# Expert hidden activations turned on VectorE instead of TensorE, and the final-row work moved around them

## The chip, the cores and the metric

The kernel runs on one core of one Trainium2 chip. The core has five engines with a queue each: TensorE (PE; its weight loads are listed as PEld), VectorE (DVE), ScalarE (ACT), GpSimd (POOL) and SyncE (SP). Engines run their own instructions in order and meet at semaphores. The metric is device time in microseconds (us) of one launch. The kernel before took 2361.81 us, the median of three runs (2359.26, 2361.81, 2366.89).

## The reference, cut to what matters

One encoder layer is applied to two groups of 1024 rows of width 1024. Its last part is an expert-choice mixture: each of 16 experts picks 128 rows of each group.

```python
gate, idx = lax.top_k(aff.T, cap)                 # cap = 128 rows of a group, for each expert
xe = xf[idx]
hid = silu(xe @ w_gate[e]) * (xe @ w_up[e])       # per expert, 1024 wide
ye = (hid @ w_down[e]) * gate
y = zeros.at[idx].add(ye)                         # rows of all experts added up
x = x + gate2 * rmsnorm(y)                        # the final rows
```

All matrices are f32. The kernel splits each operand into a high and a low part and forms each product from three matmuls (high by high, low by high, high by low).

## The kernel before, in words

The function `experts` covers the second half of the time, from about 1283 us on. It runs experts 0 to 15 in turn; the first eight stand in a loop, the last eight are written out. Both groups are worked on together: 128 rows of each.

**Weights.** An expert has three matrices, called GATE, UP and DOWN, and each comes in four pieces of 1 MB. Four buffers hold pieces. SP loads a piece (`moe_wf`), ACT copies its high part (`moe_w_hi`, line 2404), DVE subtracts to get the low part (`moe_w_lo`, line 2553), and PE multiplies with both (line 2734). A "split" is the ACT copy and the DVE subtraction of one piece. A buffer is free for the next split when PE has finished the piece four places earlier.

**Order on PE** in the body of expert e: UP(e), GATE(e+1), DOWN(e), twelve pieces of 24 matmuls. GATE(e+1) waits for the turned and split inputs of expert e+1 (`x_ready`, `moe_x_lo`, line 2573).

**Hidden activations.** ACT writes silu of the GATE sums to `hid`, DVE multiplies them by the UP sums (line 2598). DOWN needs `hid` turned, rows against columns. For experts 0 to 7 DVE turns it with 16 transposes (line 2581), ACT and DVE then split it from SBUF (lines 2423 and 2587), and PE does the high parts of DOWN's first piece ahead of the low parts (`down_first`, line 2766). For experts 8 to 15 (`is_late`) PE turns it with 16 transposes in the midst of GATE(e+1) (line 2754), and ACT and DVE split it out of PSUM (lines 2411 and 2559).

**Inputs of an expert.** POOL gathers the rows of expert e+2 with eight indirect DMAs (line 2308), DVE turns them (line 2568). POOL also adds an expert's output rows to `scratch_y` in HBM with two indirect DMAs (line 2325, the "scatter").

**Final rows.** 26 units of 128 rows are finished while experts 9 to 15 still run, four to an expert (two in expert 15), in pairs. For a unit POOL loads rows of y and of x1 (lines 2337 and 2338; 2341 and 2342 where the rows are picked by an index), ACT sums the squares (line 2458, it waits for the y load), DVE makes the mean (2602), POOL the root (2352), DVE the result (2610 and 2616, the latter waits for the x1 load), and POOL stores it (2359, by index 2365). Units 0 to 15 are plain rows, units 16 to 25 go by index. Units use buffers 0 and 1 in turn; a load waits until the store two units earlier has landed. A POOL body starts when the scatter of the expert before has landed: loads of the first pair, gather of one group, roots, stores, then the same for the second pair, then the scatter. Units 26 and 27, the rows of expert 15, end the kernel.

Of the kernel before, what the change touches and what calls it, by code (L numbers as in the profile page):

```python
# [8 lines left out]
ALU = mybir.AluOpType  # L9
# [24 lines left out]
ONE = 1  # L34
# [2054 lines left out]
def experts(nc, io):  # L2089
# [5 lines left out]
    NP = KC // PIECE  # L2095
# [8 lines left out]
    LATE = 8  # L2104
# [15 lines left out]
    with ExitStack() as ctx:  # L2120
# [64 lines left out]
        late_h_turned, late_h_hi_ready, late_h_ready = (s.sem(f"late_h_{n}") for n in ("turned", "hi_ready", "ready"))  # L2185
# [46 lines left out]

        def is_late(e):
            return isinstance(e, int) and e >= LATE

# [29 lines left out]
        def _(pool):  # L2265
# [65 lines left out]
            def load_unit(n):  # L2331
# [4 lines left out]
                if t is not None:  # L2336
                    pool.dma_start(fy[:, j, :], y_view[t]).then_inc(fy_loaded[j], 16)
                    pool.dma_start(fx[:, j, :], x1_view[t]).then_inc(fx_loaded[j], 16)
                else:
                    at = bass.IndirectOffsetOnAxis(ap=index_c[:, col(e, g)], axis=0)  # L2340
                    pool.indirect_dma_start(fy[:, j, :], None, io["y"], at).then_inc(fy_loaded[j], 16)  # L2341
# [8 lines left out]
            def root(n):  # L2350
                pool.wait_ge(y_mean, n + 1)
                nc.gpsimd.tensor_tensor(y_r[:, n % 2:n % 2 + 1], y_ss[:, n % 2:n % 2 + 1], mhalf[:, :], ALU.pow).then_inc(y_root, 1)
# [44 lines left out]
        def _(act):  # L2397
# [27 lines left out]
            def silu(e, j, bs=range(BK)):  # L2425
# [4 lines left out]
                if len(bs) == BK and is_late(e - 1):  # L2430
                    act.wait_ge(late_h_turned, ONE + (e - LATE) * BK)
                elif len(bs) == BK:
                    act.wait_ge(h_turned, ONE + e)
# [38 lines left out]
            def body(e, j):  # L2472

                ns = window(e)
                if is_last(e):
                    split(e, DOWN, range(0, 2))
                    turned_out(e - LATE, (h_hi, j), late_h_turned, late_h_hi_ready, range(0, 2))
# [3 lines left out]
                    turned_out(e - LATE, (h_hi, j), late_h_turned, late_h_hi_ready, range(2, BK))  # L2481
                else:
# [30 lines left out]
        def _(dve):  # L2513
# [119 lines left out]
            def body(e, j):  # L2633
                ns = window(e)
                if is_last(e):
                    multiply(e, j, range(0, 2))
                    split(e, DOWN, range(0, 2))
                    turned_out(e - LATE, h_hi, h_lo, j, late_h_hi_ready, late_h_ready, range(0, 2))
                    multiply(e, j, range(2, BK))
                    split(e, DOWN, range(2, NP))  # L2640
                    for n in ns:
                        mean(n)
                    turned_out(e - LATE, h_hi, h_lo, j, late_h_hi_ready, late_h_ready, range(2, BK))
                    for n in ns:
                        result(n)
                else:
# [3 lines left out]
                    if is_late(e):  # L2650
                        split(e + 1, GATE, range(2, NP))
                        multiply(e, j)
                    else:
                        split(e + 1, GATE, range(2, 3))
                        multiply(e, j)
                        split(e + 1, GATE, range(3, NP))
                        turn_h(e)
                    split(e, DOWN, range(0, 1))
                    if not is_late(e):
                        h_out(e)  # L2660
                    for n in ns[0:2]:
                        mean(n)
                    split(e, DOWN, range(1, 2))
                    if is_late(e):
                        turned_out(e - LATE, h_hi, h_lo, j, late_h_hi_ready, late_h_ready)
# [232 lines left out]
```

## Time and profile before

| | us |
|---|---|
| median of three runs | 2361.81 |
| the profiled execution | 2362.63 |
| its span, first to last instruction | 2360.9 |
| PE busy | 2255.7 (96%) |
| DVE busy | 1349.1 (57%) |
| ACT busy | 1100.5 (47%) |
| POOL busy | 730.6 (31%) |

Times in rows count from the start of the span. The profiled execution's own time is 1.7 us more than its span. A row of the timeline gives the start, the duration, engine, line, what is written from what, and in brackets the idle time of that engine before it with what ended it. A DMA's row on POOL tells how long POOL took to issue it, not when the data landed; landing times stand in the views of one line.

### The profile page before, as it was taken

Reading aid. Unit: us, or ns where it says so; the run is one execution under the profiler, and the core shown is the slowest. Engines: PE = TensorE matmul, PEld = TensorE weight load, DVE = VectorE, ACT = ScalarE, POOL = GpSimd, SP = SyncE. Lnnn points to the kernel's source line nnn. Section 1 sums busy time; section 2 is a strip of 40 time slices with the busy share of each in tenths; the row PEclk is TensorE's granted clock in tenths of the full one; section 3 lists DMA queues with packets and bytes.
Section 4 is the critical chain, followed back from the end, with each engine's and each line's share of the span. In section 5 each row is a group of like instructions: output and inputs, shape, how many; then the busy total and the mean of one; then the engine's idle time right before and its main releaser. Section 6 shows DMA issues by size and latency. Waiting matters only on the chain. (4 is left out here: it accounts for less than half of the span.)

```text
span 2360.9 us, 34620 instructions
## 1 busy us (share of the span) xinstructions
PE 2255.7 (96%) x13219; PEld 1876.9 (79%) x13219; DVE 1349.1 (57%) x1995; ACT 1100.5 (47%) x1782; POOL 730.6 (31%) x770
## 2 busy tenths in 40 slices
PE   6999999999999999999984999999999999999997
PEld 4679989867899898677763888888888888888885
DVE  3212344555422436665557877777777667677665
ACT  4212434555534436665542544544444455545552
POOL 3004241434233515340003222221222333443634
PEclk9999999999999999999996999999999999999998
DMA  8745445657554459764538666766667678988785
GB/s 314 265 114 184 153 148 192 188 137 185 139 188 152 148 172 247 225 183 162 169 128 313 215 218 231 248 223 224 209 224 244 229 267 316 334 311 302 286 304 178
DMA packets 224095, 511.49 MB, mean 217 GB/s; under 512 B 38420, under 2 KB 129444, under 8 KB 204496
## 3 DMA queue, kind: packets, MB, share of 16 engines
q1 hardware_dynamic: 174576, 394.78, 49.3%
q0 software_dynamic: 49376, 114.78, 16.5%
q8 instruction: 92, 1.51, 0.3%
q14 instruction: 51, 0.42, 0.1%
HBM read 415.32 MB, written 93.69 MB: 216 GB/s over the span
## 5 line engine op out<-in xcount | busy, mean ns | idle before, releaser
L2553 DVE TENSOR_TENSOR moe_w_lo<-moe_wf,moe_w_hi 128x2048 fp32r<-128x2048 f32 x192 | 437.2, 2288 | 252.4 <-ACT moe_w_hi L2404 251.5
L2404 ACT ACTIVATE moe_w_hi<-moe_wf 128x2048 fp32r<-128x2048 f32 x192 | 366.0, 1915 | 436.7 <-PE moe_acc L2734 424.1
L2734 PE MATMUL moe_acc<-moe_w_hi,moe_x_hi 128*128 128x512 f32 x1024 | 400.1, 391 | 2.9 <-DVE moe_w_lo L2553 2.0
L2734 PE MATMUL moe_acc<-moe_w_lo,moe_x_hi 128*128 128x512 f32 x1024 | 399.2, 390 | 0.0
L2734 PE MATMUL moe_acc<-moe_w_hi,moe_x_lo 128*128 128x512 f32 x1024 | 399.1, 390 | 0.0
L2734 PEld LDWEIGHTS moe_acc<-moe_w_hi,moe_x_hi 128*128 128x128 f32 x1024 | 192.6, 188 | 43.7 <-DVE moe_w_lo L2553 2.4
L2734 PEld LDWEIGHTS moe_acc<-moe_w_hi,moe_x_lo 128*128 128x128 f32 x1024 | 192.6, 188 | 40.1
L2734 PEld LDWEIGHTS moe_acc<-moe_w_lo,moe_x_hi 128*128 128x128 f32 x1024 | 192.5, 188 | 39.7
L1793 PE MATMUL banks<-fr_w_hi,fr_h_hi 128*128 128x256 f32 x768 | 223.2, 291 | 0.0
L1793 PE MATMUL banks<-fr_w_lo,fr_h_hi 128*128 128x256 f32 x768 | 217.0, 283 | 0.0
L1793 PE MATMUL banks<-fr_w_hi,fr_h_lo 128*128 128x256 f32 x768 | 216.9, 282 | 0.0
L2308 POOL DMA_INDIRECT moe_xe<-scratch_h,moe_parts x120 | 181.5, 1513 | 86.8 <-issue 77.3
L1784 PE MATMUL banks<-fr_h_hi,fr_w_hi 128*128 128x512 f32 x496 | 204.3, 412 | 1.9 <-DVE fr_h_lo L1381 1.1
L1784 PE MATMUL banks<-fr_h_hi,fr_w_lo 128*128 128x512 f32 x496 | 194.2, 392 | 0.0
L1784 PE MATMUL banks<-fr_h_lo,fr_w_hi 128*128 128x512 f32 x496 | 193.7, 391 | 0.0
L1030 ACT ACTIVATE fr_stage<-banks 128x512 f32<-128x512 f32 (+1 forms) x114 | 67.4, 591 | 270.9 <-PE banks L1784 145.8
L1362 DVE TENSOR_TENSOR fr_w_lo<-fr_w_raw,fr_w_hi 128x1024 fp32r<-128x1024 f32 x56 | 71.2, 1274 | 209.3 <-ACT fr_w_hi L1018 209.3
L906 POOL DMA_DIRECT2D fr_v<-scratch_vov x224 | 156.2, 746 | 81.9 <-PE banks L1963 80.5
L2734 PE MATMUL moe_acc<-moe_w_hi,moe_h_hi 128*128 128x512 f32 x448 | 174.4, 389 | 0.0
L2734 PE MATMUL moe_acc<-moe_w_hi,moe_h_lo 128*128 128x512 f32 x448 | 174.3, 389 | 0.0
L2734 PE MATMUL moe_acc<-moe_w_lo,moe_h_hi 128*128 128x512 f32 x448 | 174.3, 389 | 0.0
L1793 PEld LDWEIGHTS banks<-fr_w_hi,fr_h_hi 128*128 128x128 f32 x768 | 146.8, 191 | 4.9 <-issue 4.8
(312 smaller groups left out, 4306.7 us busy)
## 6 DMA issues: line engine op xcount, KB each, us to landing
moe_wf<-in_w_expert_gate SPq DMA_DIRECT2D x64, 1024.0 KB, 5.3
moe_wf<-in_w_expert_up SPq DMA_DIRECT2D x64, 1024.0 KB, 6.0
moe_wf<-in_w_expert_down SPq DMA_DIRECT2D x64, 1024.0 KB, 6.8
fr_w_raw<-in_w_units SPq DMA_DIRECT2D x28, 1024.0 KB, 6.7
fr_bias<-in_na_bias SPq DMA_DIRECT2D x16, 1520.0 KB, 11.7
fr_a_w<-in_w_ada POOLq DMA_DIRECT2D x16, 1024.0 KB, 8.4
scratch_qk_t<-fr_stage SPq DMA_DIRECT2D x64, 256.0 KB, 2.5
scratch_vov<-fr_stage SPq DMA_DIRECT2D x96, 128.0 KB, 2.4
```

Source lines behind the costliest of these rows:

```text
L906: pool.dma_start(v[j][p0:CHUNK, CH_AT[rb] + n, :], v_view[2, m, r0:r0 + k, cols_, :]).then_inc(nv_loaded[j], 16)
L1030: nc.scalar.activation(out, product, ACT.Copy).then_inc(evac_done, 1)
L1362: nc.vector.tensor_tensor(w_lo[:, h % 2, k, :], w_raw[:, h % 2, k, :], w_hi[:, h % 2, k, :].bitcast(F32), ALU.subtract).then_inc(w_lo_read ...
L1784: mm = nc.tensor.matmul(ps[:, b % 2, :], w[x1][:, slot, k, a * P:(a + 1) * P], h[x2][:, k, t * HALF:(t + 1) * HALF], start=start, stop=stop)
L1793: mm = nc.tensor.matmul(ps[:, b % 2, part * QW:(part + 1) * QW], h[x1][:, k, tile:tile + P], w[x2][:, slot, k, :], start=(k == 0 and i == ...
L2308: pool.indirect_dma_start(quarter_rows(g)[:, t, :], None, h2_quarters, bass.IndirectOffsetOnAxis(ap=at, axis=0)).then_inc(gathered[g], 16)
L2404: nc.scalar.activation(w_hi[:, q, :, :], wf[:, q, :, :], ACT.Copy).then_inc(w_hi_ready, 1)
L2553: nc.vector.tensor_tensor(w_lo[:, q, :, :], wf[:, q, :, :], w_hi[:, q, :, :].bitcast(F32), ALU.subtract).then_inc(w_lo_ready, 1)
L2734: mm = nc.tensor.matmul(acc[:, j, b, :], x[:, g, k, :], w[:, q, a, h * HALF:(h + 1) * HALF], start=(k == 0 and i == 0), stop=(k == KC - 1 ...
```

## The change

`LATE` and `is_late` go: experts 8 to 14 turn `hid` as experts 0 to 7 do, by DVE, and PE transposes it for expert 15 alone. The rest moves the work on final rows. POOL's gather of both groups comes first in the body, before the wait for the scatter. A pair's two y loads are issued together, and without waiting for the stores of the pair before; the x1 loads follow, with that wait. On ACT and DVE the squares, means and results of a pair stand one split later.

```diff
-                if not ns and not is_last(e, 2):
+                if not is_last(e, 2):
                     gather(e + 2, j)
                 if ns:
                     pool.wait_ge(added, (ZEROS + e * GROUPS) * 16)
-                    for h, half in enumerate((ns[0:2], ns[2:4])):
+                    for half in (ns[0:2], ns[2:4]):
                         for n in half:
-                            load_unit(n)
-                        if not is_last(e, 2):
-                            gather(e + 2, j, range(h, h + 1))
+                            load_y(n)
+                        for n in half:
+                            load_x1(n)
```

`load_y` has no wait; `load_x1` begins with the old one:

```diff
+            def load_x1(n):
+                j = n % 2
+                g, t, e = units[n]
+                if n >= 2:
+                    pool.wait_ge(out_stored[j], 16 * (n // 2))
```

ACT, body of an expert that is not the last:

```diff
                     split(e, DOWN, range(0, 1))
-                    if not is_late(e):
-                        h_out(e)
+                    h_out(e)
+                    split(e, DOWN, range(1, 2))
                     for n in ns[0:2]:
                         square(n)
-                    split(e, DOWN, range(1, 2))
-                    if is_late(e):
-                        turned_out(e - LATE, (h_hi, j), late_h_turned, late_h_hi_ready)
                     split(e, DOWN, range(2, NP))
 
                     silu(e + 1, 1 - j)
-                    split(e + 1, UP, range(0, 2))
+                    split(e + 1, UP, range(0, 3))
                     for n in ns[2:4]:
                         square(n)
-                    split(e + 1, UP, range(2, NP))
+                    split(e + 1, UP, range(3, NP))
```

DVE, the end of the same body:

```diff
                     for n in ns[0:2]:
                         result(n)
-                    split(e, DOWN, range(2, NP))
-                    split(e + 1, UP, range(0, 2))
+                    split(e, DOWN, range(3, NP))
+                    split(e + 1, UP, range(0, 3))
                     for n in ns[2:4]:
                         mean(n)
+                    split(e + 1, UP, range(3, NP))
                     for n in ns[2:4]:
                         result(n)
-                    split(e + 1, UP, range(2, NP))
```

PE, the same body:

```diff
-                    products(e + 1, GATE, 1 - j, x_hi[:, 1 - j], x_lo[:, 1 - j], first)
-                    if is_late(e):
-                        turn_h(e, j)
-                    products(e + 1, GATE, 1 - j, x_hi[:, 1 - j], x_lo[:, 1 - j], second)
-                    if is_late(e):
-                        pe.wait_ge(late_h_ready, ONE + (e - LATE) * BK + BK)
-                        products(e, DOWN, j, h_hi, h_lo)
-                    else:
-                        down_first(e, j)
-                        products(e, DOWN, j, h_hi, h_lo, range(1, NP))
+                    products(e + 1, GATE, 1 - j, x_hi[:, 1 - j], x_lo[:, 1 - j])
+                    down_first(e, j)
+                    products(e, DOWN, j, h_hi, h_lo, range(1, NP))
```

In the last expert DVE's means of its two units come behind the split of the second half of `hid` instead of ahead of it; ACT's squares stay ahead of that half's copy out of PSUM.

Where it moves instructions, first on DVE around `hid` of a late expert. Before, from the multiplication (`moe_hid`) on; `moe_w_lo` is a weight split, `moe_parts` the means, `moe_h_lo` the split of the turned `hid`:

```order
L2598 TENSOR_TENSOR moe_hid<-moe_hid,moe_acc 128x512 x4
L2553 TENSOR_TENSOR moe_w_lo<-moe_wf,moe_w_hi 128x2048
L2602 TENSOR_SCALAR moe_parts<-moe_parts 128x1 x2
L2553 TENSOR_TENSOR moe_w_lo<-moe_wf,moe_w_hi 128x2048
L2559 TENSOR_TENSOR moe_h_lo<-moe_acc,moe_h_hi 128x512 x4
```

Now, at the same place (lines lie one lower):

```order
L2597 TENSOR_TENSOR moe_hid<-moe_hid,moe_acc 128x512 x4
L2552 TENSOR_TENSOR moe_w_lo<-moe_wf,moe_w_hi 128x2048
L2580 STREAM_TRANSPOSE moe_h_raw<-moe_hid 32x16x32 x16
L2552 TENSOR_TENSOR moe_w_lo<-moe_wf,moe_w_hi 128x2048
L2586 TENSOR_TENSOR moe_h_lo<-moe_h_raw,moe_h_hi 128x1024 x2
L2552 TENSOR_TENSOR moe_w_lo<-moe_wf,moe_w_hi 128x2048
L2601 TENSOR_SCALAR moe_parts<-moe_parts 128x1 x2
```

Sixteen transposes have come in, the split of `hid` is two instructions on SBUF instead of four on PSUM, and the means stand behind a weight split more.

Second, DVE at the end of the body, from DOWN's last splits to the turn of the next expert's inputs (`moe_x_raw`). Before:

```order
L2553 TENSOR_TENSOR moe_w_lo<-moe_wf,moe_w_hi 128x2048 x4
L2602 TENSOR_SCALAR moe_parts<-moe_parts 128x1 x2
L2610 SCALAR_TENSOR_TENSOR moe_fy<-moe_fy,moe_parts,moe_rows 128x1024
L2616 TENSOR_TENSOR moe_fx<-moe_fx,moe_fy 128x1024
L2610 SCALAR_TENSOR_TENSOR moe_fy<-moe_fy,moe_parts,moe_rows 128x1024
L2616 TENSOR_TENSOR moe_fx<-moe_fx,moe_fy 128x1024
L2553 TENSOR_TENSOR moe_w_lo<-moe_wf,moe_w_hi 128x2048 x2
L2568 STREAM_TRANSPOSE moe_x_raw<-moe_xe 128x4x8x32 x2
```

Now:

```order
L2552 TENSOR_TENSOR moe_w_lo<-moe_wf,moe_w_hi 128x2048 x4
L2601 TENSOR_SCALAR moe_parts<-moe_parts 128x1 x2
L2552 TENSOR_TENSOR moe_w_lo<-moe_wf,moe_w_hi 128x2048
L2609 SCALAR_TENSOR_TENSOR moe_fy<-moe_fy,moe_parts,moe_rows 128x1024
L2615 TENSOR_TENSOR moe_fx<-moe_fx,moe_fy 128x1024
L2609 SCALAR_TENSOR_TENSOR moe_fy<-moe_fy,moe_parts,moe_rows 128x1024
L2615 TENSOR_TENSOR moe_fx<-moe_fx,moe_fy 128x1024
L2567 STREAM_TRANSPOSE moe_x_raw<-moe_xe 128x4x8x32 x2
```

The second pair's two results stand between the body's last weight split and the turn of the next inputs; two weight splits stood there.

Third, POOL in expert 13, whose units go by index: loads (`moe_fy` is y, `moe_fx` is x1), gather (`moe_xe`), roots (`moe_parts`), stores (`out`). Before:

```order
L2341 DMA moe_fy<-scratch_y,moe_parts 128x1024
L2342 DMA moe_fx<-scratch_x,moe_parts 128x1024
L2341 DMA moe_fy<-scratch_y,moe_parts 128x1024
L2342 DMA moe_fx<-scratch_x,moe_parts 128x1024
L2308 DMA moe_xe<-scratch_h,moe_parts 128x256 x4
L2352 TENSOR_TENSOR moe_parts<-moe_parts 128x1 x2
L2365 DMA out<-moe_fx,moe_parts 2048x1024 x2
```

Now:

```order
L2304 DMA moe_xe<-scratch_h,moe_parts 128x256 x8
L2334 DMA moe_fy<-scratch_y,moe_parts 128x1024 x2
L2345 DMA moe_fx<-scratch_x,moe_parts 128x1024 x2
L2356 TENSOR_TENSOR moe_parts<-moe_parts 128x1 x2
L2369 DMA out<-moe_fx,moe_parts 2048x1024 x2
```

The whole gather is ahead of the loads, and the y loads are next to each other.

## Rows read from the trace of the kernel before

**Rows 1.** The page, busy time of each engine, share and instructions.

```profile
PE 2255.7 (96%) x13219; PEld 1876.9 (79%) x13219; DVE 1349.1 (57%) x1995; ACT 1100.5 (47%) x1782; POOL 730.6 (31%) x770
```

**Rows 2.** Chain that ended last, from 1840 us: start, us, what.

```profile
1861.34 1.75 PE moe_acc L2754 x16
1863.09 65.31 PE moe_acc L2734 x288
```

**Rows 3.** Waits of PE from 1861 us on: total us, times, longest.

```profile
PE moe_acc L2734 <- DVE moe_w_lo L2553: 2.0, 1, 2.0
```

**Rows 4.** Timeline of PE at the start of UP(15) and at its stall.

```profile
2297.98 0.39 PE L2734 MATMUL moe_acc<-moe_w_hi,moe_x_hi 128*128 128x512 f32 x1
...
2305.56 0.61 PE L2734 MATMUL moe_acc<-moe_w_hi,moe_x_hi 128*128 128x512 f32 x1 [1.98 <-DVE moe_w_lo L2553]
...
2309.55 0.40 PE L2734 MATMUL moe_acc<-moe_w_lo,moe_x_hi 128*128 128x512 f32 x1
```

**Rows 5.** Busy us by stretch (PE, PEld, DVE, ACT, POOL), clock, DMA share, GB/s.

```profile
1632.60:1697.90 65.30, 65.30 (x290) 54.07 (x289) 49.40 (x38) 30.84 (x24) 16.06 (x13) 1.00 0.67 225
...
2263.70:2330.80 67.10, 65.12 (x298) 53.83 (x295) 40.95 (x33) 33.10 (x34) 31.23 (x18) 0.97 0.71 242
```

**Rows 6.** Timeline of DVE in expert 5, whose UP starts at 1632.6.

```profile
1637.06 4.19 DVE L2568 STREAM_TRANSPOSE moe_x_raw<-moe_xe 128x1024 f32<-128x1024 f32 x2
...
1645.73 2.29 DVE L2553 TENSOR_TENSOR moe_w_lo<-moe_wf,moe_w_hi 128x2048 fp32r<-128x2048 f32 x1 [2.31 <-ACT moe_w_hi L2404]
1647.93 2.35 DVE L2573 TENSOR_TENSOR moe_x_lo<-moe_x_raw,moe_x_hi 128x1024 fp32r<-128x1024 f32 x2
...
1654.66 2.48 DVE L2598 TENSOR_TENSOR moe_hid<-moe_hid,moe_acc 128x512 f32<-128x512 f32 x4 [1.14 <-PE moe_acc L2734]
...
1659.43 11.45 DVE L2581 STREAM_TRANSPOSE moe_h_raw<-moe_hid 32x512 f32<-32x512 f32 x16
...
1673.12 2.35 DVE L2587 TENSOR_TENSOR moe_h_lo<-moe_h_raw,moe_h_hi 128x1024 fp32r<-128x1024 f32 x2
```

**Rows 7.** Timeline of DVE, a result's first half, then last halves of three pairs.

```profile
2002.10 1.28 DVE L2610 SCALAR_TENSOR_TENSOR moe_fy<-moe_fy,moe_parts,moe_rows 128x1024 f32<-128x1024 f32 x1
...
2207.15 1.23 DVE L2616 TENSOR_TENSOR moe_fx<-moe_fx,moe_fy 128x1024 f32<-128x1024 f32 x1
...
2277.34 1.23 DVE L2616 TENSOR_TENSOR moe_fx<-moe_fx,moe_fy 128x1024 f32<-128x1024 f32 x1
...
2302.08 1.23 DVE L2616 TENSOR_TENSOR moe_fx<-moe_fx,moe_fy 128x1024 f32<-128x1024 f32 x1
```

**Rows 8.** Timeline of ACT: a weight split and a square.

```profile
2019.10 1.92 ACT L2404 ACTIVATE moe_w_hi<-moe_wf 128x2048 fp32r<-128x2048 f32 x1 [3.52 <-PE moe_acc L2734]
2021.10 1.06 ACT L2458 ACTIVATE moe_zero<-moe_fy 128x1024 f32<-128x1024 f32 x1
```

**Rows 9.** Line 2337, the 14 plain y loads from 1937 to 2146 us.

```profile
DMA to landing us min/median/max: 5.8/7.7/10.4
```

**Rows 10.** Timeline of POOL behind the first pair of experts 13 and 14.

```profile
2208.66 2.77 POOL L2365 DMA_INDIRECT out<-moe_fx,moe_parts  x1 [0.68 <-DVE moe_fx L2616]
2211.73 2.76 POOL L2341 DMA_INDIRECT moe_fy<-scratch_y,moe_parts  x1 [0.30 <-issue]
...
2281.92 1.90 POOL L2341 DMA_INDIRECT moe_fy<-scratch_y,moe_parts  x1 [0.30 <-issue]
```

**Rows 11.** Line 2341, landing of the loads issued at 2211.73 and 2281.92.

```profile
DMA to landing us min/median/max: 11.5/11.5/11.5
...
DMA to landing us min/median/max: 9.7/9.7/9.7
```

**Rows 12.** Timelines of POOL and DVE at the end.

```profile
2321.17 2.40 POOL L2341 DMA_INDIRECT moe_fy<-scratch_y,moe_parts  x1 [8.83 <-DMA scratch_y<-moe_ye,moe_parts]
...
2334.97 1.11 POOL L2352 TENSOR_TENSOR moe_parts<-moe_parts 128x1 f32<-128x1 f32 x2
...
2349.93 1.28 DVE L2703 SCALAR_TENSOR_TENSOR moe_ye<-moe_fy,moe_parts,moe_ye 128x1024 f32<-128x1024 f32 x1 [0.76 <-POOL moe_parts L2352]
```

More of the change, by code:

```diff
@@ L2103, in experts @@
     FIRST, UNITS = 8, 4
-    LATE = 8
     units = [(t // TT, t, None) for t in range(GROUPS * TT)]
@@ L2184, in experts @@
         hid_ready = s.sem("hid_ready")
-        late_h_turned, late_h_hi_ready, late_h_ready = (s.sem(f"late_h_{n}") for n in ("turned", "hi_ready", "ready"))
+        last_h_turned, last_h_hi_ready, last_h_ready = (s.sem(f"last_h_{n}") for n in ("turned", "hi_ready", "ready"))
         h_turned = s.sem("h_turned")
@@ L2231, in quarter_rows @@
             return xe[:, g, :].rearrange("p (t n) -> p t n", t=4)
-        def is_late(e):
-            return isinstance(e, int) and e >= LATE
         def is_last(e, n=1):
@@ L2329, in _, with load_y @@
             gather(1, 1)
-            def load_unit(n):
+            def load_y(n):
+                j = n % 2
+                g, t, e = units[n]
+                if t is not None:
+                    pool.dma_start(fy[:, j, :], y_view[t]).then_inc(fy_loaded[j], 16)
+                else:
+                    at = bass.IndirectOffsetOnAxis(ap=index_c[:, col(e, g)], axis=0)
+                    pool.indirect_dma_start(fy[:, j, :], None, io["y"], at).then_inc(fy_loaded[j], 16)
+            def load_x1(n):
                 j = n % 2
@@ L2350, in root @@
             def root(n):
+                mean = y_ss[:, n % 2:n % 2 + 1]
                 pool.wait_ge(y_mean, n + 1)
-                nc.gpsimd.tensor_tensor(y_r[:, n % 2:n % 2 + 1], y_ss[:, n % 2:n % 2 + 1], mhalf[:, :], ALU.pow).then_inc(y_root, 1)
+                nc.gpsimd.tensor_tensor(y_r[:, n % 2:n % 2 + 1], mean, mhalf[:, :], ALU.pow).then_inc(y_root, 1)
             def store_unit(n):
@@ L2429, in silu @@
                     act.wait_ge(piece_done, ONE + piece(e, GATE, NP))
-                if len(bs) == BK and is_late(e - 1):
-                    act.wait_ge(late_h_turned, ONE + (e - LATE) * BK)
-                elif len(bs) == BK:
+                if len(bs) == BK:
                     act.wait_ge(h_turned, ONE + e)
@@ L2476, in body @@
                     split(e, DOWN, range(0, 2))
-                    turned_out(e - LATE, (h_hi, j), late_h_turned, late_h_hi_ready, range(0, 2))
+                    turned_out(0, (h_hi, j), last_h_turned, last_h_hi_ready, range(0, 2))
                     split(e, DOWN, range(2, NP))
@@ L2480, in body @@
                         square(n)
-                    turned_out(e - LATE, (h_hi, j), late_h_turned, late_h_hi_ready, range(2, BK))
+                    turned_out(0, (h_hi, j), last_h_turned, last_h_hi_ready, range(2, BK))
                 else:
@@ L2637, in body @@
                     split(e, DOWN, range(0, 2))
-                    turned_out(e - LATE, h_hi, h_lo, j, late_h_hi_ready, late_h_ready, range(0, 2))
+                    turned_out(0, h_hi, h_lo, j, last_h_hi_ready, last_h_ready, range(0, 2))
                     multiply(e, j, range(2, BK))
                     split(e, DOWN, range(2, NP))
+                    turned_out(0, h_hi, h_lo, j, last_h_hi_ready, last_h_ready, range(2, BK))
                     for n in ns:
                         mean(n)
-                    turned_out(e - LATE, h_hi, h_lo, j, late_h_hi_ready, late_h_ready, range(2, BK))
                     for n in ns:
@@ L2649, in body @@
                     x_out(e + 1, 1 - j)
-                    if is_late(e):
-                        split(e + 1, GATE, range(2, NP))
-                        multiply(e, j)
-                    else:
[L2654 to L2657, printed above, removed]
+                    split(e + 1, GATE, range(2, 3))
+                    multiply(e, j)
+                    split(e + 1, GATE, range(3, NP))
+                    turn_h(e)
                     split(e, DOWN, range(0, 1))
-                    if not is_late(e):
-                        h_out(e)
+                    h_out(e)
+                    split(e, DOWN, range(1, 2))
                     for n in ns[0:2]:
                         mean(n)
-                    split(e, DOWN, range(1, 2))
-                    if is_late(e):
-                        turned_out(e - LATE, h_hi, h_lo, j, late_h_hi_ready, late_h_ready)
+                    split(e, DOWN, range(2, 3))
                     for n in ns[0:2]:
                         result(n)
-                    split(e, DOWN, range(2, NP))
-                    split(e + 1, UP, range(0, 2))
+                    split(e, DOWN, range(3, NP))
+                    split(e + 1, UP, range(0, 3))
                     for n in ns[2:4]:
                         mean(n)
+                    split(e + 1, UP, range(3, NP))
                     for n in ns[2:4]:
                         result(n)
-                    split(e + 1, UP, range(2, NP))
             over_experts(dve, body)
```

11 lines of the change are left out of this document (3 added, 8 removed).

## The prediction

> **What bounds the kernel now.** The busy times of the page came first: PE works 96% of the span [rows 1]. The chain of waits came next. From 1840 us it runs through PE alone, a stretch of 288 matmuls in 65.31 us and then 1.75 us for 16 transposes, five times over [rows 2]; so a matmul takes 65.31 / 288 = 0.2268 us, one of the twelve pieces of an expert 5.44 us, and a late expert 67.06 us. The reader should see that nothing stands between: the view of waits has one wait of PE behind 1861 us, 2.0 us [rows 3]. It is in UP(15): UP(15) begins at 2297.98, the gap is at 2305.56, and the ten matmuls up to 2309.55 then take 3.99 us instead of 2.27 [rows 4]. That is 1.7 us more, with a granted clock of 0.97 in that stretch against 1.00 elsewhere [rows 5], which is some matmuls at the lower of the two levels, 1.2 instead of 2.4 GHz, after PE had idled. So up to expert 14 PE sets the pace, and every instruction taken off it counts in full, provided that DVE, ACT and POOL keep up. From the end of PE's work a tail of DVE and POOL steps follows [rows 12].
>
> **PE: what goes.** Experts 8 to 14 lose 16 transposes each: 7 x 1.75 = 12.2 us, all on the path. That the other form costs PE nothing by itself shows in expert 5, which turns by DVE: PE is busy 65.30 of 65.30 us there [rows 5].
>
> **DVE in an expert with final rows.** I lay it out in time t from the start of UP(e) on PE: GATE(e+1) begins at 21.8, DOWN(e) at 43.5, the next UP at 65.3. Expert 5 started at 1632.6 (expert 8's transposes at 1861.34, less six pieces and three experts). There the inputs' turn starts at t = 4.5, their low parts end at 17.7, the 16 transposes (11.45 us) end at 38.3, the low parts of `hid` at 42.9 [rows 6]. Now two results, 2 x (1.28 + 1.23) = 5.0 us [rows 7], stand ahead of that turn. The turn then ends at 13.7, two weight splits at 18.1, and the low parts of the inputs at 20.4; the 2.31 us that DVE idled there in expert 5 [rows 6] takes up part. PE wants them at 21.8: 1.3 us of cover. Behind it, a split (22.6) and the multiplication (25.0, half a microsecond behind expert 5's) put the low parts of `hid` at 43.4, and `down_first` wants them only after two thirds of a piece, at 47.2. This part costs nothing, and is bounded by the 1.3 us: any delay of the second results beyond it is a wait of PE.
>
> **Where the second results stand.** The split of DOWN's second piece ends at 45.7. ACT's copies of the high parts (from t = 38.3), that copy, two squares and the third piece's copy (1.92 and about 1.25 us each [rows 8]) let DVE end its third split at 49.7, and the first pair's results at 54.7. POOL stores, then loads y for the second pair without a wait. ACT can start the squares when its copy for UP's third piece is done, at 61.9 (eleven pieces of PE and 1.92), and must end them by 65.4, when DOWN is done and the last copy can start.
>
> For plain rows (units 0 to 15, experts 9 to 12) the two y loads go out at 55.7 and 56.2 (1 us behind the result) and land in 5.8 to 10.4 us, median 7.7 [rows 9]: the second at 63.9, its square done at 65.2. In time: 0 us. With the longest landing it is 2.5 us late, 1.2 us beyond the cover, four times 4.8 us.
>
> **Expert 13, where rows go by index.** The trace has the same step in both of its pairs: last result done at 2208.38 and 2278.57 [rows 7], y load issued 3.35 us later [rows 10], landed 11.5 and 9.7 us after that [rows 11]. So y is there 14.9 or 13.1 us behind the result; I take the mean, 14.0. The second y load is issued right behind, 2.76 + 0.3 us later while DVE works on weight splits [rows 10]; I let it land 3.1 us behind the first. That is 54.7 + 14.0 + 3.1 = 71.8. Square 1.3 (73.1), copy 1.92 (75.0), split 2.29 (77.3), results 5.0 (82.3), turn, two splits and low parts 11.0 (93.3). PE wants GATE(15)'s inputs at 65.3 + 21.8 = 87.1: it waits 6.2 us, and the clock costs 1.7 as behind the gap of before. 7.9 us given back, in the body of expert 14. Its bounds are 0 (y there by 64, as for plain rows) and 10 (y 2 us later). Before, the same square came late as well, and its result is the gap in [rows 4]; but a weight split's delay had three pieces of cover; now the turn of the inputs is behind it, with 1.3 us.
>
> **Expert 14 and the last expert.** PE's expert 14 lasts 65.3 + 7.9 = 73.2. DVE's low parts of the inputs end at 28.0, the first results 34.3 later (20.4 to 54.7 above) at 62.3, and units 22 and 23 by the same steps at 89.9, which is 16.7 behind the start of UP(15). Before they were done at 2303.31, 5.3 behind it [rows 4, 7]. So the last stores, and the scatter of expert 14 queued behind them on POOL, go out 11.4 us later. Before, 17.9 us passed from there to the first load of expert 15, 13.8 to the roots, 16.2 to the end of the last result at 2351.21 [rows 12]; all in all 53.2 behind the start of UP(15). At worst the tail grows by 11.4. Less, because POOL's eight loads would cost 0.95 + 0.3 each beside an idle DVE (10.0 instead of 13.8), and because the store and scatter would move with hardly a weight load in flight (I take 14.5 for the 17.9). 11.4 - 3.8 - 3.4 = 4.2 us. The best case is PE's own: its gap and slow matmuls of 4.0 us go, -4.0. ACT's squares of units 24 and 25 stand ahead of the copy of `hid`'s second half, so PE waits there too; that is the same delay, not a second one.
>
> **POOL's gather first.** Eight issues, now between the scatter's issue and its landing, where POOL waited 8.83 us before [rows 12]. The first pair's loads move behind them, but their squares also move back, to t = 43; cost 0, and if the gather ran 10 us over it would be the plain-row case above.
>
> **Sum**, against the profiled execution (span 2360.9, time 2362.63, 0.8 above the median of 2361.81): -12.2 + 0 + 7.9 + 4.2 = -0.1 us, so 2362.5 for such an execution and 2361.7 for the median. I write 2361.5.
>
> **The rivals.**
>
> *The loads come in time.* If the by-index y loads land like plain ones (t = 64), expert 14 has no wait and the tail keeps PE's pace or loses a few us: -12.2 with -4.0 to +1, that is 2346 to 2351. For it: the second y load no longer waits for a store to land, and that wait stood ahead of the 1.98 us gap [rows 4]. Against it: the first y of the pair never had that store in its way, and took 9.7 and 11.5 us all the same. The Trainium skill's DMA: Bandwidth & Descriptors, section on the anatomy of one DMA on the SWDGE (gpsimd) path, fits a load at about 2.0 us plus its bytes over 436e3, 3.2 us for 512 KB, which would give this rival its time; the landings in [rows 9, 11] are two to three times that.
>
> *DVE becomes the bound (the other side).* DVE gains 11.45 us an expert, and the loop results, y load, square, split, results, turn, low parts closes in about 65 us against PE's 65.3. If plain y loads land in 10.4 instead of 7.7, PE waits in each of experts 10 to 13 for `moe_x_lo`, 1.2 us and the clock's 1.7 each: 11.6 on top of the forecast, 2373. It decides at a landing of about 9 us. For it: DMA engines are busier in a shorter expert. Against it: the median. The Trainium skill's VectorE: DVE Perf Modes, section on rules for kernel authors, would leave a 128 x 128 transpose on TensorE where PSUM will do, since VectorE turns 32 x 32 blocks only; by it the change goes this rival's way. Expert 5's rows, with DVE at 49.4 of 65.3 us and no wait of PE, speak against it where no final rows stand beside.
>
> *The change doesn't do what it says.* The order on DVE shows the 16 transposes in late experts, so I give this nothing.
>
> **How the numbers follow.** The forecast 0.54, spread over 2354 to 2371; the loads in time 0.30; DVE the bound 0.16. A difference of 0.3% (7 us) is about what can be told from none here: faster is below 2354.7, slower above 2368.9. Faster: 0.30 and 0.03 from the edge of the forecast. Slower: 0.16 and 0.05 from its other edge. The same: 0.46. The forecast's own range is 2355 to 2369; for 8 in 10 I reach into both rivals, 2350 to 2371.
>
> **What would show it.** In the profile after: stretches of 288 matmuls without transposes from 1861 us on (the 12.2); PE's waits by line with `moe_x_lo` as releaser, one of some 6 us in expert 14 and none in 9 to 12; ACT waiting for the y load ahead of the square of unit 18; expert 14's scatter some 11 us later behind the start of UP(15) than before, and PE waiting for `moe_h_lo` in the last expert. No wait for `moe_x_lo` in expert 14 would make the first rival right; waits in every expert the second.

## The result and the profile after

The changed kernel took 2364.75 us, the median of 20 runs (2360.22 to 2369.70), the kernel before 2361.07 us in 20 runs beside them: 1.0013 times as long, with a 95% interval of 1.0007 to 1.0019, so 1.7 to 4.5 us slower. Timed once more among the experiments it stood at 1.0010 (1.0001 to 1.0019). The forecast was 2361.5, a change of nothing; the time lies in its range, but the difference is real and on the slow side.

The profiled execution of it took 2362.10 us. Its page has these busy times [of before: rows 1]:

```profile
PE 2248.7 (95%) x13107; PEld 1869.4 (79%) x13107; DVE 1427.0 (60%) x2093; ACT 1097.7 (47%) x1768; POOL 738.6 (31%) x770
```

112 PE instructions are gone, the 7 x 16 transposes. Its view of PE's waits behind 1820 us has two rows, where [rows 3] have one:

```profile
PE moe_acc L2727 <- DVE moe_x_lo L2572: 6.3, 1, 6.3
PE moe_acc L2727 <- DVE moe_h_lo L2558: 5.1, 1, 5.1
```

Its timeline of PE, at the start of UP(14), at the first of these waits, in GATE(15), and at the start of UP(15):

```profile
2220.74 0.39 PE L2727 MATMUL moe_acc<-moe_w_hi,moe_x_hi 128*128 128x512 f32 x1
...
2248.97 0.80 PE L2727 MATMUL moe_acc<-moe_w_hi,moe_x_hi 128*128 128x512 f32 x1 [6.32 <-DVE moe_x_lo L2572]
2249.56 0.63 PE L2727 MATMUL moe_acc<-moe_w_lo,moe_x_hi 128*128 128x512 f32 x1
2249.99 0.63 PE L2727 MATMUL moe_acc<-moe_w_hi,moe_x_lo 128*128 128x512 f32 x1
...
2252.34 0.40 PE L2727 MATMUL moe_acc<-moe_w_hi,moe_x_lo 128*128 128x512 f32 x1
...
2294.08 0.39 PE L2727 MATMUL moe_acc<-moe_w_hi,moe_x_hi 128*128 128x512 f32 x1
```

Expert 14 lasts 73.34 us, 8.06 over the 65.28 that an expert without a wait takes here. Behind the wait the matmuls start 0.43 us apart until 2252.10 and 0.23 from then on: 1.2 GHz, then 2.4. The windows of the same execution (columns as in [rows 5]), expert 9, expert 13 and expert 14:

```profile
1894.10:1959.40 65.30, 65.30 (x290) 54.10 (x289) 54.37 (x45) 34.51 (x31) 27.05 (x23) 1.00 0.80 276
2155.20:2220.70 65.50, 65.50 (x289) 54.00 (x288) 59.05 (x49) 34.20 (x30) 37.59 (x24) 1.00 0.88 304
2220.70:2294.10 73.40, 67.08 (x290) 55.12 (x290) 59.15 (x50) 34.98 (x32) 27.71 (x19) 0.95 0.79 280
```

The chain that ended last no longer runs through PE alone [rows 2]. From expert 9 on it goes round the loop that the prediction laid out; here the turn from expert 13 to 14:

```profile
2209.59 1.24 DVE moe_fx L2615
...
2211.22 2.64 POOL out L2369
...
2214.16 1.89 POOL moe_fy L2334
...
2216.36 11.47 DMA moe_fy<-scratch_y,moe_parts
...
2229.06 1.82 ACT moe_w_hi L2408
...
2230.90 2.29 DVE moe_w_lo L2552
...
2234.46 1.23 DVE moe_fx L2615
...
2238.10 4.17 DVE moe_x_raw L2567 x2
2242.27 4.38 DVE moe_w_lo L2552 x2
2246.65 1.14 DVE moe_x_lo L2572
```

The reader should follow it: the first pair's second result, its store by index, the second pair's y load and its landing, ACT's split behind the square, DVE's split, the second pair's results, the turn of the next inputs, two weight splits, their low parts. Those end 6.3 us after PE wanted them. The same chain has the landing of the second y load of each second pair of plain rows, in experts 9 to 12:

```profile
1949.08 9.90 DMA moe_fy<-scratch_y
...
2015.27 9.57 DMA moe_fy<-scratch_y
...
2081.11 8.89 DMA moe_fy<-scratch_y
...
2146.22 9.66 DMA moe_fy<-scratch_y
```

**Stages.** More profiles of both kernels were taken (below). From the starts of UP in their PE timelines, and the span:

| execution | us | start of UP(8) | experts 8 to 13 | expert 14 | UP(15) to the end |
|---|---|---|---|---|---|
| before, the one shown | 2362.63 | 1828.54 | 402.36 | 67.08 | 62.92 |
| before, second | 2362.49 | 1830.49 | 402.36 | 67.08 | 60.77 |
| before, third | 2359.93 | 1828.27 | 402.38 | 67.08 | 60.47 |
| changed, first | 2362.10 | 1828.81 | 391.93 | 73.34 | 66.22 |
| changed, second | 2362.80 | 1828.65 | 392.28 | 73.65 | 66.42 |
| changed, third | 2364.01 | 1829.69 | 392.95 | 75.12 | 64.44 |
| changed, fourth | 2364.69 | 1829.07 | 393.68 | 73.64 | 66.51 |

Between the means stand -9.66, +6.86 and +4.51 us (+5.28 against the second and third of before alone), in all +1.7 (+2.5).

### The profile page after: what moved, and what is told of

It is laid out like the page before. It is cut to its first block and busy times, and to the rows that moved or that the text cites. A ratio compares the mean times of both kernels' runs of the same rounds, so it can differ in the third digit from the quotient of the medians.

```text
span 2360.3 us, 34481 instructions
## 1 busy us (share of the span) xinstructions
PE 2248.7 (95%) x13107; PEld 1869.4 (79%) x13107; DVE 1427.0 (60%) x2093; ACT 1097.7 (47%) x1768; POOL 738.6 (31%) x770
## 5 line engine op out<-in xcount | busy, mean ns | idle before, releaser
L2304 POOL DMA_INDIRECT moe_xe<-scratch_h,moe_parts x120 | 202.4, 1686 | 86.5 <-issue 75.7
L2580 DVE STREAM_TRANSPOSE moe_h_raw<-moe_hid 32x512 f32<-32x512 f32 x240 | 168.7, 703 | 4.5
L2727 PE MATMUL moe_acc<-moe_w_hi,moe_h_hi 128*128 128x512 f32 x392 | 153.5, 392 | 5.1 <-DVE moe_h_lo L2558 5.1
L2727 PE MATMUL moe_acc<-moe_w_lo,moe_h_hi 128*128 128x512 f32 x392 | 153.3, 391 | 0.0
L2727 PE MATMUL moe_acc<-moe_w_hi,moe_h_lo 128*128 128x512 f32 x392 | 153.1, 391 | 0.0
```

Of the source, the lines that this page charges most:

```text
L2304: pool.indirect_dma_start(quarter_rows(g)[:, t, :], None, h2_quarters, bass.IndirectOffsetOnAxis(ap=at, axis=0)).then_inc(gathered[g], 16)
L2580: a = nc.vector.transpose(h_raw[u * QT:(u + 1) * QT, :, :, t * QT:(t + 1) * QT], columns)
L2727: mm = nc.tensor.matmul(acc[:, j, b, :], x[:, g, k, :], w[:, q, a, h * HALF:(h + 1) * HALF], start=(k == 0 and i == 0), stop=(k == KC - 1 ...
```

## The experiments

All ratios are to the kernel before, timed on the same chip in the same rounds, with 95% intervals.

**1. Each part alone.** One part: the kernel before with VectorE's turn for experts 8 to 14.

```diff
-    LATE = 8
+    LATE = 15
```

> One part alone: hid of experts 8 to 14 is turned on VectorE, while the final rows keep the order of the kernel before on every engine. Theory A: 7 x 1.75 = 12.2 us leave TensorE; the second pair by index in expert 13 is late here too (its y load waits for a store besides), and two weight splits stand between its results and the turn of the next inputs, so PE waits for weight splits or inputs there: 4 to 10 us given back, in all 2352 to 2358. Rival C (what costs is the new order of the final rows, not the turn on VectorE): no wait of PE in expert 14, 2349 to 2351. Rival B (VectorE's 11.45 us more in an expert are too much beside the final rows): PE waits in several of experts 9 to 14, 2364 or more.

Measured: 2381.93 us, 1.0085 (1.0071 to 1.0099). PE's waits of this kernel:

```profile
PE moe_acc L2734 <- DVE moe_w_lo L2553: 20.0, 7, 9.5
PE moe_acc L2734 <- DVE moe_x_lo L2573: 6.5, 4, 1.8
```

Experts 10 to 13 last 68.3 to 69.2 us and expert 14 73.9. Rival B's picture, and my 2352 to 2358 fell: in the old order the turn costs some 19 us net of what it takes off PE, so the new order is what makes it bearable.

The other part: the new order, with hid of experts `LATE` on turned on PE; `LATE = 8` is the order alone, `LATE = 13` a mixture. On ACT:

```diff
-                    h_out(e)
+                    if not is_late(e):
+                        h_out(e)
                     split(e, DOWN, range(1, 2))
+                    if is_late(e):
+                        turned_out(e - LATE, (h_hi, j), last_h_turned, last_h_hi_ready)
                     for n in ns[0:2]:
                         square(n)
```

> The other part alone: the new order of gathers, loads, squares, means and results, while hid of experts 8 to 14 is still turned on TensorE (its copy out of PSUM stands ahead of the first pair's squares on ScalarE and ahead of the means on VectorE). Theory A: VectorE has 11.45 us more room in each expert, so the late pair of expert 13 costs no wait for moe_x_lo, or one of under 2 us; the tail is 0 to 4 us longer by the square ahead of the copy of hid in the last expert: 2359 to 2365. Rival C (the new order costs by itself): a wait for moe_x_lo of some 6 us in expert 14 as in the changed kernel, and the tail, without the 12.2 us that the turn gives: 2369 or more.

Measured: 2364.28 us, 1.0016 (1.0003 to 1.0030), from 2359.90 to 2371.60 (before 2358.26 to 2366.69 beside it), and a profile at 2360.04 without any wait of PE. The expected time, but with a spread that neither theory has; experiment 5 takes it up.

> The new order throughout, with hid turned on VectorE in experts 8 to 12 and on TensorE in 13 to 15, so that no pair of rows by index stands in a VectorE body that is full. Theory A: 5 x 1.75 = 8.8 us leave TensorE, no wait for moe_x_lo over 1 us in any expert, tail as in the kernel with the order alone: 7 to 10 us under the kernel before, 2351 to 2354. Rival B (the loop on VectorE is full with plain rows too): waits for moe_x_lo in experts 10 to 13 take back 4 us or more, 2357 or more.

Measured: 2363.80 us, 1.0002 (0.9993 to 1.0011). Theory A fell. With PE turning hid in experts 13 and 14, PE's waits are

```profile
PE moe_acc L2740 <- DVE moe_x_lo L2581: 8.2, 2, 7.3
PE moe_acc L2740 <- DVE moe_h_lo L2567: 1.9, 1, 1.9
```

0.9 us in GATE(14) and 7.3 in GATE(15). So the pair is late without transposes beside it. This execution has another cause at hand, though: in expert 13 the first gather's issue on POOL, and ScalarE's first square, whose y load stands behind that gather:

```profile
2173.00 8.92 POOL L2308 DMA_INDIRECT moe_xe<-scratch_h,moe_parts  x1 [0.30 <-issue]
...
2202.63 1.06 ACT L2466 ACTIVATE moe_zero<-moe_fy 128x1024 f32<-128x1024 f32 x1 [8.62 <-DMA moe_fy<-scratch_y,moe_parts]
```

How much of the 7.3 us comes from this wait of 8.62 us, and how much from a margin that experts 9 to 12 had used up, the run doesn't separate. Experiment 5 returns to such issues.

**2. Rows by index or plain rows.** In the changed kernel, units 18 and 19 load as plain rows (and in the second kernel units 16 to 19 are plain throughout). The rows that they write are then not the layer's; only the times are of use:

```diff
                 g, t, e = units[n]
+                if n in (18, 19):
+                    t = n
...
+    units[16:20] = [(0, t, None) for t in range(2, 6)]
```

> The changed kernel with the second pair of expert 13 (units 18 and 19) loading y and x1 as plain rows instead of rows picked by an index; their output rows are not the reference's. It takes away the long landing of loads by index in that one place. Theory A (that landing is the 7.9 us of expert 14): the wait of PE for moe_x_lo in GATE(15) falls from 6.3 us to under 1.5, units 22 and 23 come earlier by as much, and the time falls by 6 to 10 us against the changed kernel (about 2364), to 2354 to 2358. Rival B (the loop is full with plain rows already, as the margin was 0 at GATE(14)): a wait of 2 to 4 us stays in GATE(15), and the time falls by under 5 us, to 2359 or more.

Measured: 2363.66 us, 1.0011 (1.0002 to 1.0020), and expert 14 lasts 72.82 us. The wait for `moe_x_lo` is 5.4 us, more than either theory left. The two plain y loads at 2215.6 and 2216.2 land as late as those by index:

```profile
DMA to landing us min/median/max: 9.3/10.9/12.5
```

> The changed kernel with units 16 to 19 (all four of expert 13) loaded and stored as plain rows; the rows of experts 9 and 11 that they finish, and those of 10 and 12, do not get their last sums. In the kernel with plain loads for units 18 and 19 alone the y loads landed as late as those by index, 9.3 and 12.5 us, behind the two stores by index of units 16 and 17. Theory S (it is these stores, 1.8 and 2.6 us of issue and their traffic, that make the next y loads late): the y loads go out near t = 56 behind the start of UP(13) and land near 66 as in experts 10 to 12, PE's wait for moe_x_lo in GATE(15) falls from 6.3 us to under 1.5, and the time falls by 6 us or more, to 2354 to 2358. Rival B (the loop is full, whatever the form of rows): a wait of 3 us or more stays, 2360 or more.

Measured: 2362.56 us, 1.0000 (0.9989 to 1.0011). Rival B. The wait for `moe_x_lo` in GATE(15) is 3.1 us, expert 14 lasts 71.33. By one profile each, against 73.94, the mean of the changed kernel, rows by index are worth 2.6 us, of which the second pair's loads are 1.1; 6.05 us stay with plain rows. Why the second y load takes 11.3 us to land there, and the one in expert 12 of the same execution 9.9, isn't settled.

**3. The tail.** ACT's last squares behind the copy of hid's second half:

```diff
-                    for n in ns:
-                        square(n)
                     turned_out(0, (h_hi, j), last_h_turned, last_h_hi_ready, range(2, BK))
+                    for n in ns:
+                        square(n)
```

> The changed kernel with ScalarE's squares of units 24 and 25 behind its copy of the second half of hid in the last expert, instead of ahead of it. It takes away PE's wait for moe_h_lo (5.1 us and slow matmuls behind it). If that wait is on the path that sets the end: PE ends some 7 us earlier and the time falls by 5 to 7 us, to 2357 to 2359. If the tail hangs on the y loads of units 24 and 25 (their results stand ahead of the last rows on VectorE): PE ends as much earlier, but the time falls by 1 to 3 us only, to 2361 to 2363.

Measured: 2362.34 us, 1.0006 (0.9997 to 1.0015), 0.9 to 1.7 us under the changed kernel by the ratios (1.0010 and 1.0013). PE's wait for `moe_h_lo` is gone from its profile, and UP(15) to the end takes 63.6 us. The second case: the tail hangs on the y loads of units 24 and 25. So next, besides that, expert 14's scatter goes ahead of the roots and stores in front of it, and ScalarE weighs the output rows ahead of the squares of units 22 and 23; on POOL:

```diff
+                        if half == ns[2:4] and e in DEFER + EARLY:
+                            for n in half:
+                                pool.wait_ge(fy_loaded[n % 2], 16 * (n // 2 + 1))
+                            scatter(e, j)
```

> As the kernel before this one, and in expert 14 GpSimd issues the scatter as soon as the y loads of units 22 and 23 have landed, ahead of their roots and stores (ScalarE weighs the output rows ahead of these squares). So the loads of units 24 and 25 go out some 10 to 13 us earlier. If the tail hangs on those loads: it ends with PE, 5 to 8 us under the changed kernel, 2356 to 2359, and the last result ends some 49 to 51 us behind the start of UP(15), where it was 56.4 in the changed kernel and 53.2 in the kernel before. If the tail has another bound: within 2 us of the kernel with the copy first.

Measured: 2357.78 us, 0.9978 (0.9969 to 0.9987). As expected: POOL's scatter and the load behind it in this kernel, against 2313.73 and 2324.19 in the changed one:

```profile
2301.19 1.86 POOL L2327 DMA_INDIRECT scratch_y<-moe_ye,moe_parts  x1 [4.26 <-ACT moe_ye L2465]
...
2317.24 1.49 POOL L2375 DMA_INDIRECT out<-moe_fx,moe_parts  x1 [6.96 <-DMA out<-moe_fx,moe_parts]
2319.03 0.97 POOL L2340 DMA_INDIRECT moe_fy<-scratch_y,moe_parts  x1 [0.30 <-issue]
```

The last result ends 49.95 us behind the start of UP(15) (56.4 in the changed kernel, 53.2 in the profile shown of before). The gain is smaller than 10 us in the loads, since the second store by index waits 6.96 us for the first to land and the loads stand behind it.

**4. The loop cut.** Second pair of experts 9 to 13 put off into the next body; on DVE:

```diff
                     x_out(e + 1, 1 - j)
+                    for n in old:
+                        result(n)
                     split(e + 1, GATE, range(2, 3))
```

> The changed kernel with the second pair's work put off into the next expert in experts 9 to 13: squares behind the weighing of the output rows on ScalarE, means and results behind the low parts of the next inputs on VectorE, roots and stores behind the scatter on GpSimd. The loop results, y load, square, split, results, turn, low parts is cut. Theory A (only the pair by index of expert 13 costs): the wait of PE for moe_x_lo goes, 7 to 10 us under the changed kernel, 2354 to 2357, and no more than that. Rival B (the loop costs in plain experts too in typical executions): over 10 us, under 2354. Rival D (VectorE is too full between the low parts of the inputs and those of hid: by the durations of the trace 28.2 us of work in 29.5): PE waits for moe_h_hi or moe_h_lo in each of experts 10 to 14, 0.5 to 3 us, and the time is 2358 or more.

Measured: 2359.58 us, 0.9996 (0.9987 to 1.0005). No wait for `moe_x_lo` is left; UP(15) starts at 2288.47, 5.6 us before that of the changed kernel's first profile (counted from UP(8), 7.4 us before the mean of the four), and in place of rival D's waits there is one of 1.5 us, for a weight split in DOWN(14). But the time falls by less, 3.3 to 4.0 us by the ratios, as the tail has become 69.3 us: units 22 and 23 are ready at 2305.7, only 3.5 us earlier. So I had the size of the gain at UP(15), and missed that the tail doesn't follow the start of UP(15). With both cures:

> The second pair put off into the next expert (experts 9 to 13) together with the early scatter of expert 14 and the copy of hid ahead of the last squares. If the two places are independent: UP(15) starts near 2288.5 us as in the kernel with the results behind, and from there the tail takes the 60 us of the kernel with the early scatter, a span of 2348 to 2350, a time of 2349 to 2353, 9 to 12 us under the kernel before. Rival (the tail hangs on the y loads of units 22 and 23, which come no earlier): 2354 to 2358.

Measured: 2353.48 us, 0.9966 (0.9953 to 0.9979), 8 us under before and faster than both kernels. PE's waits of this kernel behind 1820 us:

```profile
PE moe_acc L2792 <- DVE moe_w_lo L2574: 1.5, 1, 1.5
PE moe_acc L2780 <- DVE moe_hid L2619: 1.4, 1, 1.4
```

UP(15) starts at 2288.78 as expected; the tail is 62.2 us instead of 60, so part of the rival holds: the time lies between the two ranges.

**5. What spreads the times.**

> The changed kernel unchanged, for a second profile and the size of its variation. Theory A (the pair of rows picked by index in expert 13 is late, nothing else): 3 to 5 us above the kernel before; the waits of PE for moe_x_lo stay one, in expert 14, but it is longer than the 6.3 us of the first profile where the execution is longer, and the last expert's wait for moe_h_lo stays one. Rival B (VectorE has become the bound, as the loop results, y load, square, split, results, turn, low parts has no cover left): in an execution that takes about 2365 us or more, waits for moe_x_lo of 0.5 to 2 us show in one or more of experts 10 to 13 too, each with slow matmuls behind it.

> The changed kernel unchanged, one more profile. If waits for moe_x_lo in experts 10 to 13 make the difference between its executions: the time above or below 2362 goes with the sum of these waits and of the one in expert 14 (8.06 us from UP(14) to UP(15) over 65.28 in the first profile). If the front half or the tail makes it: these waits are the same within 0.3 us, and the start of UP(8) or the stretch behind UP(15) differs.

> As the run before this one: one more profile of the changed kernel, to see in which stretch its executions differ.

Measured: 2362.80, 2364.01 and 2364.69 us, the executions of the table (the first is one of eleven runs, median 2363.45). The drift in experts 9 to 13, over six times 65.28 us, is 0.25, 0.60, 1.27 and 2.00 us in the four, in the order of their times. The fourth has its first wait in GATE(13), of plain rows:

```profile
2113.29 0.50 PE L2727 MATMUL moe_acc<-moe_w_hi,moe_x_hi 128*128 128x512 f32 x1 [1.18 <-DVE moe_x_lo L2572]
```

Rival B, then, though small: the waits ahead of expert 14's are of 0.21 to 1.18 us, and no slow matmuls follow them.

> The kernel before unchanged, a second profile. If the forecast's baseline was untypical: an execution near 2361 us has no gap in UP(15), or one under 1 us without slow matmuls, and its stretch from UP(15) to the end is 1 to 4 us under the 62.9 us of the first profile. If it was typical: the same gap of about 2 us, 62.5 to 63.5 us, and the difference between executions lies ahead of UP(8).

> As the run before this one, a third profile of the kernel before.

Measured: 2362.49 and 2359.93 us. Both have the gap in UP(15), 1.51 and 1.15 us long, and none of the slow matmuls that follow it in [rows 4]. The timeline of PE in the third execution of before:

```profile
2304.47 0.50 PE L2734 MATMUL moe_acc<-moe_w_hi,moe_x_hi 128*128 128x512 f32 x1 [1.15 <-DVE moe_w_lo L2553]
2304.81 0.39 PE L2734 MATMUL moe_acc<-moe_w_lo,moe_x_hi 128*128 128x512 f32 x1
2305.04 0.39 PE L2734 MATMUL moe_acc<-moe_w_hi,moe_x_lo 128*128 128x512 f32 x1
```

Starts 0.23 apart from the second on. Their tails are 60.77 and 60.47 us, 2.2 to 2.5 under the execution shown. The gaps are over the 1 us that I had named for an untypical baseline, the tails are as I had said.

> The order alone once more (hid turned on TensorE in experts 8 to 14). If its first profile, 2360.0 us without any wait of PE, was a short execution: one of 2364 us or more shows 2 to 8 us of waits for moe_x_lo or moe_w_lo behind UP(13), or a tail over 63 us. If the spread (2359.9 to 2371.6) is of the front half: the start of UP(8) is 1830 us or later. The median stays within 2 us of 2364.

> The order alone, a third profile. A long execution (2364 us or more) shows waits of PE of 3 us or more in all behind UP(8), or a stretch behind UP(15) over 64 us; if it shows neither, the front half is what differs.

> As the run before this one, a fourth profile of the order alone.

> As the run before this one, a fifth profile of the order alone.

Measured: 2370.09 us in six runs, 1.0035 (1.0022 to 1.0047), which misses the median that I gave; the profiles took 2362.17, 2373.11, 2360.71 and 2361.84 us. The long one has 6.7 us of waits for `moe_x_lo`, 5.9 of them in GATE(15), and an expert 14 of 75.70 instead of 67.08; the others have none. POOL in expert 12 of the long one, the scatter and the first two gathers:

```profile
2112.53 1.59 POOL L2325 DMA_INDIRECT scratch_y<-moe_ye,moe_parts  x1 [0.30 <-issue]
2114.42 8.96 POOL L2308 DMA_INDIRECT moe_xe<-scratch_h,moe_parts  x1 [0.30 <-issue]
2123.68 0.99 POOL L2308 DMA_INDIRECT moe_xe<-scratch_h,moe_parts  x1 [0.30 <-issue]
```

The same place in the first profile of this kernel:

```profile
2108.60 1.59 POOL L2325 DMA_INDIRECT scratch_y<-moe_ye,moe_parts  x1 [0.30 <-issue]
2110.49 2.26 POOL L2308 DMA_INDIRECT moe_xe<-scratch_h,moe_parts  x1 [0.30 <-issue]
2113.06 1.84 POOL L2308 DMA_INDIRECT moe_xe<-scratch_h,moe_parts  x1 [0.30 <-issue]
```

And DVE in the long one, from just ahead of that issue:

```profile
2113.54 4.44 DVE L2561 TENSOR_TENSOR moe_w_lo<-moe_wf,moe_w_hi 128x2048 fp32r<-128x2048 f32 x2
2117.91 2.34 DVE L2581 TENSOR_TENSOR moe_x_lo<-moe_x_raw,moe_x_hi 128x1024 fp32r<-128x1024 f32 x2
2120.18 2.27 DVE L2561 TENSOR_TENSOR moe_w_lo<-moe_wf,moe_w_hi 128x2048 fp32r<-128x2048 f32 x1
2122.38 2.46 DVE L2606 TENSOR_TENSOR moe_hid<-moe_hid,moe_acc 128x512 f32<-128x512 f32 x4
```

The issue begins in the first of five subtractions of two SBUF operands that follow each other without a gap, and ends a microsecond after the last. In the short case it gets in between the first two. ScalarE then waits 9.52 us for the first y load behind the gather in the long execution, and not for that load in the short one. Long issues (8.92 to 8.98 us) stand in experts 11, 12 and 13 of the long execution, none in the first two profiles, one in each of the last two. The changed kernel has three, three, two and two in its four profiles, and one of 4.44 us, which gets in behind the second subtraction; the profiles of before have no issue over 3 us there, and the kernels with the results behind have none, whose gather stands behind the roots. That three in a row make the 8.6 us is the reading of one execution, no run having moved the gather alone. In the changed kernel the drift is not theirs: in all four profiles the y loads of every first pair land 2.6 us or more ahead of their squares, for which ScalarE never waits (though the view of the first profile's chain leads through the gather in experts 10, 11 and 13), and the profiles with fewer long issues drift more. What goes with the drift there is the second y load of the second pairs: in the fourth profile the one of expert 11, ahead of the wait in GATE(13), took 11.27 us to land, where the first had 8.89.

## Why the prediction was wrong

**The transposes, -12.2: right.** Experts without a wait take 65.28 instead of 67.06 us, 12.5 for seven.

**Expert 14, +7.9: right in size, 8.06 in the first profile and 8.66 in the mean of four.** The step's times hold to a microsecond: the second y load landed at 72.6 behind UP(13) (71.8 forecast). The reason that I gave it, the landing by index, is only a part: with plain rows 6.05 us stay. The rest is a loop without cover left and a landing of 11.3 us on plain rows, whose length stays open (experiment 2).

**Plain rows, 0: the first step that failed.** It let the second y load land in 7.7 us, the median of [rows 9], and so kept 1.3 us of cover for `moe_x_lo`. But that median mixes the two loads of a pair. In expert 10 of the kernel before, the second pair's first and second load:

```profile
DMA to landing us min/median/max: 6.5/6.5/6.5
...
DMA to landing us min/median/max: 10.4/10.4/10.4
```

The second ones took 9.7 to 10.4 us in experts 9 to 12 before, and 8.9 to 11.3 in the four profiles of the changed kernel, at or over the 9 us at which the prediction said that its second rival decides. The four profiles drift by 1.03 us in the mean. So this rival, DVE as the bound, was at work in plain experts, at a tenth of its price. The prediction did not see the held gather either: it took 2.76 us as the worst price of an issue beside VectorE [rows 10], and the move put it where it can be 8.97. But no square of a first pair waited for it (experiment 5).

**The tail, +4.2: too small, and by another path.** The changed kernel's tail has 65.90 us in the mean, 3.0 over the 62.92 from which I counted, so by its own count the step was over the mark. But that 62.92 held a 1.98 us gap and eight steps of 0.40 to 0.43 us from matmul to matmul, which I took for the kernel's. Two more executions of before have gaps of 1.51 and 1.15 us and no such steps: their 60.6 make the tail +5.3. The difference of 0.8 us between that execution and the median, which I allowed, was 1.56 against 20 runs.

The path was another one, too. The prediction counted from the last stores over POOL's loads and roots to the last result, and called that a tail behind PE's work. The last matmul of before, then the last matmul and the last result of the changed kernel (before's last result is in [rows 12]):

```profile
2346.99 0.39 PE L2734 MATMUL moe_acc<-moe_w_hi,moe_h_lo 128*128 128x512 f32 x1
...
2346.23 0.39 PE L2727 MATMUL moe_acc<-moe_w_hi,moe_h_lo 128*128 128x512 f32 x1
...
2349.17 1.28 DVE L2696 SCALAR_TENSOR_TENSOR moe_ye<-moe_fy,moe_parts,moe_ye 128x1024 f32<-128x1024 f32 x1 [0.76 <-POOL moe_parts L2356]
```

PE works until 3.8 us before the last result, in all three profiles of before and all four of the changed kernel. So what holds PE in the last expert sets the end: the gap before, and now the wait for `moe_h_lo`, which comes from the y loads of units 24 and 25. Without that wait (the copy first) PE ends 8.3 us ahead of the last result, and the loads' own path sets the end instead.

Together, against typical executions: -10.69 + 1.03 for experts 8 to 13, -1.80 + 8.66 for expert 14, +5.28 for the tail, +2.5 us, in the measured 1.7 to 4.5. The loop and its wait in expert 14 were as forecast; three terms were too small by about 1 us each (plain rows 1.03, expert 14 0.8, the tail 1.1), all on the slow side, and no one of them alone brings the sum into that interval. The forecast of nothing was a sum of larger terms that happened to cancel. The first rival, loads in time, fell: no profile is without the wait in expert 14. PE's wait for `moe_h_lo` in the last expert came as forecast (5.1 us), and was nearly no second delay, as forecast: removing it gave 0.9 to 1.7 us.

## What to carry to other kernels

Work taken off the engine that sets the pace pays only if every loop through the others closes in less than the new period: here a loop of VectorE, GpSimd, a DMA and ScalarE took some 65 us, and cutting it (results behind the next inputs' low parts, the scatter ahead of the stores) turned a loss of 0.13% into a gain of 0.34%. Where an expected difference is a few microseconds, take the base of each stage from several executions: one gap with slow matmuls in the only profile was worth 2.2 to 2.5 us, more than the whole forecast. Where a step hangs on the last of several loads, take its landing from the last ones, not from a median of all. Before moving a GpSimd DMA, look at what VectorE runs just then.

## What the runs showed of the hardware

An indirect DMA's issue on GpSimd can be held through a whole run of five VectorE subtractions with two SBUF operands, 8.92 to 8.98 us, at a place where in other executions it takes 2.22 to 2.27 us and once took 4.44. The Trainium skill's SBUF — State Buffer, section SBUF: two separate sides, says that VectorE and GpSimd share a port pair as an exclusive lock, held for the whole instruction. The rows agree that one blocks the other, and show more: five instructions in a row can keep it.

After idle gaps of 1.51 us and 1.15 us TensorE's matmuls went on at 0.23 us, 2.4 GHz; after 1.98 us eight steps were 0.40 to 0.43, after 6.32 us six behind the first, 1.2 GHz.
